# Order of the small work in five stages of a twelve-stage transformer kernel: retention scores, mask loads, a second pair's values, a memory's low parts, the dilated divisions, and three projection steps

## What is computed

```python
x = first_block(x)     # neighbourhood attention, swiglu, dilated attention, swiglu
for l in range(2):     # second block
    x = x + 0.5 * rms_norm(swiglu(rms_norm(x)))
    if l == 0:
        p = h @ ev_w_in
        y_a = rwkv7_mix(p[..., :RW_IN])          # delta rule, 8 heads of 64
        y_b = retention_mix(p[..., RW_IN:])      # 4 heads of 128, rotary, decay mask
        h = concatenate([y_a, y_b]) @ ev_w_out
    else:
        h = concatenate([dsa_mix(p), short_conv_mix(p)]) @ od_w_out
    x = x + rms_norm(h)
    x = x + rms_norm(memory_xattn(rms_norm(x), mem_n))   # 4 heads, keys and values from a memory
    x = x + 0.5 * rms_norm(swiglu(rms_norm(x)))
```

## Time and profile before

| | |
|---|---|
| median of three runs (lowest, highest) | 1929.08 us (1928.88, 1930.92) |
| the profiled execution: its time, its span | 1927.48 us, 1925.7 us |
| granted clock, mean of the span | 0.995 |
| weight stream: loads, KB each, median us to landing | 301, 1024.0, 4.8 |
| transfers over the span | 338.13 MB, 176 GB/s |
| chain that ended last, by engine | PE 62%, DVE 13%, ACT 11%, issue 9% |

### The profile page before, as it was taken

The page is one execution under the profiler, slowest core; times in us unless marked ns, Lnnn a source line. Parts: engine busy times, 40 slices in busy tenths (PEclk is TensorE's granted clock), DMA queues, the critical chain, the costliest instruction groups (busy, mean ns, idle before and its releaser), DMA issues.

```text
span 1925.7 us, 38585 instructions
## 1 busy us (share of the span) xinstructions
PE 1864.5 (97%) x15800; PEld 1761.9 (91%) x15800; DVE 1339.8 (70%) x1814; ACT 920.9 (48%) x1255; POOL 85.0 (4%) x104
## 2 busy tenths in 40 slices
PE   8999999999989999999999999999999999899998
PEld 8989989999979998999998888999899988799997
DVE  6867756766777775776677677777577667677774
ACT  5554445444454444444436454444444444555442
POOL 2300000000000000000000010000000003100000
PEclk9999999999999999999999999999999999999999
DMA  7445564443525564556541223556455652354553
GB/s 293 154 165 197 185 237 183 176 177 132 182 93 187 186 229 174 188 183 233 216 173 53 112 94 148 189 185 228 174 191 183 234 206 110 121 186 153 177 204 131
DMA packets 50099, 338.13 MB, mean 176 GB/s; under 512 B 6080, under 2 KB 7232, under 8 KB 10560
## 3 DMA queue, kind: packets, MB, share of 16 engines
q1 hardware_dynamic: 45072, 319.74, 45.8%
q10 hardware_dynamic: 4912, 16.71, 2.4%
HBM read 335.38 MB, written 1.05 MB: 175 GB/s over the span
## 4 chain that ended last, share of the span: by engine, by line
PE 62%; DVE 13%; ACT 11%; issue 9%; POOL 1%; ACTq 1%; DVEq 0%; POOLq 0%
PE pj L243 9%; PE pj L245 9%; PE pj L244 9%; ACT whi L304 9%; PE acc L250 5%; PE acc L251 5%; PE acc L252 5%; DVE wlo L311 4%; PE pj L633 3%; PE pj L250 2%; PE pj L251 2%; PE pj L252 2%; PE pj L639 2%; DVE F L890 2%; DVE F L887 1%
## 5 line engine op out<-in xcount | busy, mean ns | idle before, releaser
L311 DVE TENSOR_TENSOR wlo<-raw,whi 128x2048 fp32r<-128x2048 f32 x285 | 651.8, 2291 | 238.8 <-ACT whi L304 237.7
L243 PE MATMUL pj<-xh,whi 128*128 128x256 f32 x2672 | 739.7, 277 | 1.3 <-DVE wlo L311 0.5
L244 PE MATMUL pj<-xl,whi 128*128 128x256 f32 x2672 | 734.8, 275 | 0.0
L245 PE MATMUL pj<-xh,wlo 128*128 128x256 f32 x2672 | 734.8, 275 | 0.0
L304 ACT ACTIVATE whi<-raw 128x2048 fp32r<-128x2048 f32 x298 | 567.9, 1912 | 331.2 <-PE acc L252 142.8
L243 PEld LDWEIGHTS pj<-xh,whi 128*128 128x128 f32 x2672 | 512.8, 192 | 6.3 <-issue 2.2
L245 PEld LDWEIGHTS pj<-xh,wlo 128*128 128x128 f32 x2672 | 513.0, 192 | 0.0
L244 PEld LDWEIGHTS pj<-xl,whi 128*128 128x128 f32 x2672 | 512.9, 192 | 0.1
L250 PE MATMUL acc<-whi,AR 128*128 128x512 f32 x656 | 253.9, 387 | 3.8 <-DVE AR L1449 3.3
L251 PE MATMUL acc<-whi,AR 128*128 128x512 f32 x656 | 249.6, 381 | 0.0
L252 PE MATMUL acc<-wlo,AR 128*128 128x512 f32 x656 | 249.4, 380 | 0.0
(11 more groups left out here) (398 smaller groups left out, 2196.3 us busy)
## 6 DMA issues: line engine op xcount, KB each, us to landing
raw<-in_wstream SPq DMA_DIRECT2D x301, 1024.0 KB, 4.8
F<-in_gains ACTq DMA_DIRECT2D x12, 512.0 KB, 4.3
XM<-in_memtok ACTq DMA_DIRECT2D x2, 1024.0 KB, 4.9
XM<-in_memin ACTq DMA_DIRECT2D x2, 1024.0 KB, 7.8
F<-in_rpb ACTq DMA_DIRECT2D x3, 512.0 KB, 3.8
F<-in_small ACTq DMA_DIRECT2D x1, 1536.0 KB, 9.4
F<-in_xin SPq DMA_DIRECT2D x2, 512.0 KB, 6.4
xt<-in_xtok SPq DMA_DIRECT2D x1, 1024.0 KB, 11.7
```

The source lines that it names most:

```text
L243: nc.tensor.matmul(o, wh, k_hi, start=first, stop=False, skip_group_check=True)
L244: nc.tensor.matmul(o, wh, k_lo, start=False, stop=False, skip_group_check=True)
L245: return nc.tensor.matmul(o, wl, k_hi, start=False, stop=last, skip_group_check=True)
L311: nc.vector.tensor_tensor(wlo[:, gs, :], raw[:, gs, :], whi[:, gs, :].bitcast(F32), ALU.subtract).then_inc(w_lo, 1)
```

## The change

No arithmetic is added or left out; pieces stand in another place of their engine's order, and one wait is added.

- Stage 1: `fill(1)` takes 23 projection steps for 20, `fill(4)` 13 for 16.
- Stage 3: chunk 26 is evacuated after iteration 9 and no longer after 8. The divisions of units 11 to 15 stand before `finish` and before the halves of the late low part (`ahead`), that of unit 10 before the evacuation of chunk 26. Before the first `first_half` PE waits for the evacuation of all projection chunks (`pj_free`); the code is shared, so stage 1 has that wait too.
- Stage 6: the retention scores stand between the two halves of chunk 10; the six mask loads are issued behind the second tanh.
- Stages 7 and 11: the second pair's values stand between the second and the third product of the last block of the first output chunk (a new hook, `amid`).
- Stage 10: `mem_low` stands right behind `mem_mean`, ahead of the low part of the second weight chunk.

```diff
@@ out_pe @@
                         x = mm3t(ob[b][:, :], whi[:, gs, wk], wlo[:, gs, wk], AR[:, kt, tt],
                                  AR[:, lo_at + kt, tt], c == 0 and kk == 0, False)
+                        if kk == 1 and b == 1:
+                            amid(pe, c)
                     if kk == 0:
                         inside(pe, c)
@@ mixer @@
-                       6: (19, 20), 7: (21, 22, 23), 8: (24, 25, 26)})
-            STEPS = {-1: 22, -2: 22, 0: 20, 1: 20, 2: 20, 3: 24, 4: 16} if na else \
+                       6: (19, 20), 7: (21, 22, 23), 8: (24, 25), 9: (26,)})
+            STEPS = {-1: 22, -2: 22, 0: 20, 1: 23, 2: 20, 3: 24, 4: 13} if na else \
...
-                {8: {10: ("front", 26), 11: ("back", 26)}}
+                {9: {10: ("front", 26), 11: ("back", 26)}}
@@ first_half @@
                     pe.wait_ge(w_lo, w.g + c + 1)
+                    if kt == 0:
+                        pe.wait_ge(pj_free, w.p + 3)
                     pe.wait_ge(*at(tag, "od", kt + 1))
@@ mixer, attn_dve @@
-                         busy=[u for u in range(4 * UP) if len(chunks_behind(u))], ahead=(5, 6) if na else (),
+                         busy=[u for u in range(4 * UP) if len(chunks_behind(u))], ahead=(5, 6) if na else range(10, 15),
@@ xattn, PE @@
-                def behind(pe, c):
+                def last_values(pe, c):
                     values(2)
                     values(3)
-                out_pe(pe, w, 4, 8, tag, "od", nxt, behind, inside=between)
+                out_pe(pe, w, 4, 8, tag, "od", nxt, inside=between, amid=last_values)
@@ dsa, DVE @@
                     if c == 0:
                         mem_mean(dve, nmt)
-                    elif c == 1:
                         mem_low(dve, nmt, mem_order)
-                    else:
+                    elif c == 2:
                         bcast_dve(dve, nmt, rM[:, :])
@@ rwrt, PE @@
-                    elif c == 9:
-                        pe.wait_ge(Sx("rot"), 4)
-                        for h, bank in enumerate((acc[2], acc[3], acc[0], mb)):
...
+                def retention_scores():
+                    pe.wait_ge(Sx("rot"), 4)
+                    for h, bank in enumerate((acc[2], acc[3], acc[0], mb)):
...
                         tile_fm(bank, 0, slot)
-                        if c == 13:
+                        if c == 10:
+                            retention_scores()
+                        elif c == 13:
                             low_rank()
@@ rwrt, ACT @@
                             nc.scalar.activation(KK[:, i, :], K_[:, i, :], ACT.Copy, scale=v("k_k", i))\
                                 .then_inc(Sx("kk"), 1)
-                        by_kind = c_dram("amask").rearrange("p (a n) -> p a n", n=P)
-                        for hc in halves:
-                            act.dma_start(AMASK[hc, 0, :], by_kind[hc, 0, hc]).then_inc(Sx("masks"), 16)
...
                 nc.scalar.activation(XWG[:, 1, :], XWG[:, 1, :], ACT.Tanh, scale=0.5).then_inc(Sx("sxg"), 1)
+                by_kind = c_dram("amask").rearrange("p (a n) -> p a n", n=P)
+                for hc in halves:
+                    act.dma_start(AMASK[hc, 0, :], by_kind[hc, 0, hc]).then_inc(Sx("masks"), 16)
...
                 act.wait_ge(Sx("lr"), 1)
```

More of the change, by code:

```diff
@@ L504, in out_pe @@
         def out_pe(pe, w, nk, lo_at, tag, ready, nxt, beside=lambda pe, c: None, fill=keep_busy, kt0=0,
-                   ob=acc, early=0, inside=lambda pe, c: None, alternate=False):
+                   ob=acc, early=0, inside=lambda pe, c: None, alternate=False, amid=lambda pe, c: None):
             post = tag + "post"
@@ L2011, in pe_f @@
                 slices_pe(pe, w)
+                def retention_scores():
+                    pe.wait_ge(Sx("rot"), 4)
+                    for h, bank in enumerate((acc[2], acc[3], acc[0], mb)):
+                        for st in range(2):
+                            last = nc.tensor.matmul(bank[:, st * T:(st + 1) * T], RK[:, h, tt(st)], RQ[:, h, :],
+                                                    start=True, stop=True)
+                        last.then_inc(Sx("rs"), 1)
                 def low_rank():
@@ L2566, in beside @@
                                 .then_inc(Sx("kk"), 1)
-                        by_kind = c_dram("amask").rearrange("p (a n) -> p a n", n=P)
-                        for hc in halves:
-                            act.dma_start(AMASK[hc, 0, :], by_kind[hc, 0, hc]).then_inc(Sx("masks"), 16)
-                            act.dma_start(AMASK[hc, 1:3, :], by_kind[hc, 2:4, hc]).then_inc(Sx("masks"), 16)
-                        act.dma_start(AMASK[:, 3:5, :].rearrange("p a n -> p (a n)"), by_kind[:, 1, :]).then_inc(Sx("masks"), 16)
-                        act.dma_start(LEV.rearrange("p a n -> p (a n)"), c_dram("levels")).then_inc(Sx("masks"), 16)
                 act.wait_ge(Sx("h0"), 1)
@@ L2593, in act_f @@
                 nc.scalar.activation(XWG[:, 1, :], XWG[:, 1, :], ACT.Tanh, scale=0.5).then_inc(Sx("sxg"), 1)
+                by_kind = c_dram("amask").rearrange("p (a n) -> p a n", n=P)
+                for hc in halves:
+                    act.dma_start(AMASK[hc, 0, :], by_kind[hc, 0, hc]).then_inc(Sx("masks"), 16)
+                    act.dma_start(AMASK[hc, 1:3, :], by_kind[hc, 2:4, hc]).then_inc(Sx("masks"), 16)
+                act.dma_start(AMASK[:, 3:5, :].rearrange("p a n -> p (a n)"), by_kind[:, 1, :]).then_inc(Sx("masks"), 16)
+                act.dma_start(LEV.rearrange("p a n -> p (a n)"), c_dram("levels")).then_inc(Sx("masks"), 16)
                 act.wait_ge(Sx("lr"), 1)
```

## The result

The changed kernel took 1913.67 us (median of four runs, 1911.17 to 1916.54), the kernel before 1929.16 beside it: a ratio of 0.9918, 95% interval 0.9901 to 0.9935. So 15.5 us less; 1912.2 was forecast, in a range of 1909.5 to 1916.5. The profiled execution is the longest of the four, 1916.54 us, with a span of 1914.8 and a mean granted clock of 0.994.

A forecast was written before the change was run, and what follows sets the result against it. TensorE, busy for 97% of the span, was taken as the bound, with time in its idle and lower clock; 2.1 + 2.1 + 4.8 + 2.7 + 2.6 + 2.6 = 16.9 us off 1929.08 gives 1912.2, range 1909.5 to 1916.5.

The forecast's parts named there:

- First stage: Three projection steps moved ahead of TensorE's first wait for L1153, and the second wait gone whole: 1.0 + 1.1 = 2.1 us.
- Dilated stage: Third stage: three softmax waits, 4.1 us, go, but 2.0 returns from chunk 26's evacuation and late low weights: 2.1 us gained.
- Retention scores: Sixth stage: half of chunk 10 first fills the rotation wait, and scores run at full clock: 13.2 us becomes 8.4, gain 4.8.
- TensorE reaches the scores just as the rotation is done: Sixth stage: after half of chunk 10 (2.68 us) TensorE is at the scores at 999.05; the last rotation ends at 998.98.
- Masks: Sixth stage: mask loads behind the second tanh cut the low-rank wait by 1.0 us; full clock gives 1.75; gain 2.7.
- The rival in which the clock falls there: The clock still falls before the low-rank products, 1.6 us of idle being left: 1.75 us less gain, 1914.0 us; chance 0.18.
- the late masks: Rival: mask loads issued later arrive too late for VectorE, so the kernel is slower, 1933 us or more; chance 0.02.
- Memory's low parts: Tenth stage: the memory's low parts fill VectorE's 2.62 us idle, so TensorE's wait for x shrinks: 2.6 us.
- Memory attentions: Two memory attentions: values leave TensorE's queue six matmuls earlier, 1.29 us each, twice 2.6; 0.35 of each wait stays.
- Half-clock stretches elsewhere move: Rival: later work shifts against whatever sets the clock, one stretch costing 2.1 us: 1910.1 or 1914.3 us; chance 0.08.
- one of my signs of being wrong: The forecast is wrong if the waits in the edited places go and the span falls by less than 12 us.

## Why the prediction was right

- **First stage** (2.1): 2.03. Three steps ran in front of the first wait, the second went whole.
- **Dilated stage** (2.1): 2.39, but for another reason than I gave. I let the evacuation of chunk 26 take part: shorten the first wait and come back as others. The runs show that it carries nothing. The divisions alone remove the two waits for L770, 2.3 us and their margins; moving the evacuation only breaks the first wait, of 1.33, into three of together 1.4.
- **Retention scores** (4.8): 4.36. The forecast was too large because two prices were too small: the scores, 3.1 from L1976's busy time, took 3.37, and the second half of the chunk took 2.87 (998.69 to 1001.56) for 2.68. The step "TensorE reaches the scores just as the rotation is done" held.
- **Masks** (2.7): 2.60, with the clock kept at a wait of 1.6, in eight of eight profiles that have it. The rival in which the clock falls there did not come, nor the late masks. The reason that I gave was luck: I inferred it from the 2.3 us wait before L358, which had kept the clock in the one profile that I had, and that same wait lost it in two of five. Why the low-rank products keep it after 1.6 us is open. The Trainium skill's rule on early issue ("DMA: Bandwidth & Descriptors", section "Rules for kernel authors") would have left the loads where they were; here the later issue cost nothing.
- **Memory's low parts** (2.6): 2.70, the wait for x gone whole. **Memory attentions** (2.6): 2 times 1.30.
- **What failed** is a step that I took without writing it as a term: that all other stretches keep the clock that the one profile shows. *Half-clock stretches elsewhere move* was among the rivals, at 2.1 and a chance of 0.08; the profile after lost 4.90 in the tenth stage alone, and the profile of before was the exception there. So one of my signs of being wrong came up: the span of the profiled executions fell by 10.9 us, less than 12, with all the waits gone. The executions of before lose such stretches too, as their mean clocks (0.992 to 0.996) say, so that between the medians most of it probably cancels: they moved by 15.5 of the 16.7, and the forecast missed by 1.5 us. That the range held rests on the median of several runs; the profiled execution itself, at 1916.54 us, lies just outside it. The Trainium skill ("TensorE: Matmul & The Clock Gate", section "What's actually happening") has the clock watched by something that runs free of the kernel; that agrees with runs of one program whose mean clock goes from 0.994 to 0.997, though no run here shows the watch itself, and I had weighed the rule at one wait where it bore on all of them.

## What to carry to other kernels

Where one engine is busy from end to end, a wait is worth its idle plus what the clock loses behind it. The idle can be read from one trace; the clock has to be read from several executions, since one profile shows only one draw of it. A small division that another engine waits for belongs ahead of a large piece that nobody waits for yet; here that held in two stages, and in the third stage moving another large piece, the evacuation, did nothing. Products that nobody reads belong ahead of the long wait: behind it, they are delay. They seem to have helped to keep the clock, but did not secure it: behind the filled wait before L1574 it fell in two of four profiles, behind the unfilled one in nine of ten.

## What the runs showed of the hardware that I had not expected

The length of a wait did not tell whether the clock fell. At 1.6 us before the low-rank products it stayed at full speed in all eight profiles; at 1.05 us before L1574 it fell in nine of ten. One and the same wait did not tell either: the 1.91 us before the seventh unit's L718 lost the clock in four of nine profiles, the 2.3 us before L358 in two of five. What else differs between these places was not tried. And at the two waits of the sixth stage the clock's share was nearly as large as the idle's: 3.3 of the 7.0 us that the stage gave, shown with the waits left in place.
